# Attention pairs of a hybrid decoder step: a projection slot placed between the second and third transposes, transposes and value products regrouped in threes

## The reference

```python
h = jnp.einsum('btd,dc->btc', xn, w_in)           # the input projection, D_MODEL = 1024
# q, k, v of the attention: 16 query heads and 2 key/value heads of 64 columns
s = jnp.einsum('bnqhgd,bnshd->bnhgqs', qb, kk).astype(jnp.float32) * scale
s = s - alibi_slopes(B_QHEADS).reshape(B_KVHEADS, B_GROUP, 1, 1) * dist
s = jnp.where(valid[None, :, None, None], s, NEG)
p = sink_softmax(s, sinks)                         # softmax with one more logit per head
o = jnp.einsum('bnhgqs,bnshd->bnqhgd', p, vv.astype(jnp.float32))
hb = ob * jax.nn.silu(zb.astype(jnp.float32))      # gated by another projection
```

## Time and profile before

| what | value |
|---|---|
| median of 3 runs | 1328.07 us (1328.01 to 1328.28) |
| profiled execution, its own time | 1327.93 us |
| its span, first to last instruction | 1326.1 us |
| PE busy | 1290.7 us (97%) |
| DVE busy | 593.1 us (45%) |
| ACT busy | 516.7 us (39%) |
| mean granted PE clock | 0.986 of full speed |

### The profile page before, as it was taken

The page is one execution under the profiler, slowest core; times in us unless marked ns, Lnnn a source line. Parts: engine busy times, 40 slices in busy tenths (PEclk is TensorE's granted clock), DMA queues, the critical chain, the costliest instruction groups (busy, mean ns, idle before and its releaser), DMA issues.

```text
span 1326.1 us, 23484 instructions
## 1 busy us (share of the span) xinstructions
PE 1290.7 (97%) x9148; PEld 1224.2 (92%) x9148; DVE 593.1 (45%) x1237; ACT 516.7 (39%) x1019; POOL 260.7 (20%) x119
## 2 busy tenths in 40 slices
PE   4999999999999999999999999999999999999998
PEld 4999999999999999999999989889888899999885
DVE  6646657474746465600000155555555202345122
ACT  6453635445353535611111354555454324114111
POOL 0222221221322222212222201111110111342000
PEclk9999999999999999999999999999999899999999
DMA  6212121302021221111112211111100312241331
GB/s 197 66 33 66 35 64 34 79 18 79 24 73 47 66 65 35 46 50 47 47 47 52 69 33 32 32 32 32 32 16 1 106 32 64 56 104 32 114 127 38
DMA packets 136750, 73.61 MB, mean 56 GB/s; under 512 B 37185, under 2 KB 133138, under 8 KB 136690
## 3 DMA queue, kind: packets, MB, share of 16 engines
q1 hardware_dynamic: 136706, 72.99, 20.0%
HBM read 63.77 MB, written 10.22 MB: 56 GB/s over the span
## 4 chain that ended last, share of the span: by engine, by line
PE 54%; DVE 4%; issue 1%; ACT 0%; DVEq 0%; ACTq 0%
PE pj L968 36%; PE pj L984 3%; PE pj L1331 3%; DVE scores L1620 2%; PE ps_e L1208 1%; PE ps_a L1331 1%; PE ps_e L1331 1%; PE ps_d L1208 1%; PE ps_a L1169 1%; PE ps_c L1331 1%; PE ps_d L1331 1%; PE ps_b L1331 1%; DVE scores L1610 1%; PE ps_c L1196 1%; PE ps_a L1196 1%; PE ps_b L1196 1%
## 5 line engine op out<-in xcount | busy, mean ns | idle before, releaser
L968 PE MATMUL pj<-xn_h,w_h 128*128 128x352 f32 x1704 | 564.6, 331 | 4.5 <-DVE xn_l L1387 1.9
L968 PE MATMUL pj<-xn_h,w_l 128*128 128x352 f32 x1704 | 553.5, 325 | 0.0
L968 PE MATMUL pj<-xn_l,w_h 128*128 128x352 f32 x1704 | 553.0, 325 | 0.0
L558 POOL TENSOR_TENSOR w_l<-w_raw,w_h 128x1024 fp32r<-128x1024 f32 x82 | 203.2, 2477 | 695.9 <-ACT w_h L630 695.9
L968 PEld LDWEIGHTS pj<-xn_h,w_h 128*128 128x128 f32 x1704 | 325.3, 191 | 13.3 <-issue 3.4
L968 PEld LDWEIGHTS pj<-xn_l,w_h 128*128 128x128 f32 x1704 | 325.6, 191 | 0.2
L968 PEld LDWEIGHTS pj<-xn_h,w_l 128*128 128x128 f32 x1704 | 325.3, 191 | 0.0
L630 ACT ACTIVATE w_h<-w_raw 128x1024 fp32r<-128x1024 f32 x82 | 86.4, 1054 | 114.4 <-PE pj L968 100.1
L1568 DVE TENSOR_TENSOR mg<-sg,pj 128x352 f32 (+1 forms) x24 | 12.4, 521 | 151.9 <-PE pj L968 150.4
L835 ACT ACTIVATE scores<-scores,stat 128x256 f32<-128x256 f32 (+1 forms) x128 | 61.4, 480 | 0.0
L968 PE MATMUL pj<-hl_l,w_h 128*128 128x352 f32 x168 | 54.2, 323 | 0.0
(11 more groups left out here) (362 smaller groups left out, 2006.9 us busy)
## 6 DMA issues: line engine op xcount, KB each, us to landing
w_raw<-in_w_in_dram SPq DMA_DIRECT2D x132, 256.0 KB, 3.4
x_t<-in_x_prompt_dram SPq DMA_DIRECT2D x8, 512.0 KB, 9.4
s<-in_state_hgrn_dram SPq DMA_DIRECT2D x8, 512.0 KB, 4.2
out_dram<-s SPq DMA_DIRECT2D x8, 512.0 KB, 3.2
w_raw<-in_w_pa_dram SPq DMA_DIRECT2D x16, 256.0 KB, 3.0
w_raw<-in_w_pb_dram SPq DMA_DIRECT2D x16, 256.0 KB, 4.4
wo_raw<-in_w_out_dram SPq DMA_DIRECT2D x8, 512.0 KB, 3.8
x_o<-in_x_prompt_dram SPq DMA_DIRECT2D x8, 512.0 KB, 4.2
```

Of the source, the lines that this page charges most:

```text
L558: g.tensor_tensor(w_l[p][:], w_raw[p][:], w_h[p][:].bitcast(F32), ALU.subtract).then_inc(w_lo_ready, 1)
L968: mm = nc.tensor.matmul(pj[g][:, 0:W], w[:, kt, :], x[:, kt, span(g)], start=(kt == 0 and m == 0), stop=(kt == KT - 1 and m == 2))
```

## The change

On PE, the slot next2 goes between t1 and t2. Behind it stand t2, t3, t4, then o0, o1; behind gate0 o2, o3, o4 and t5, t6, t7; behind gate1 o5, o6, o7. Before, the order was t0 to t2, next2, o0, o1, t3, t4, gate0, o2, o3, t5, t6, gate1, o4, t7, o5 to o7. On DVE, pt1 goes ahead of the last quarter's normalisation, and h0 ahead of pt5. On ACT, the copy q2 goes ahead of pt2, and the rounding of weights stays ahead of pt4. No instruction is added or removed.

```diff
     softmax = (["qs"] + [x for k in quarters for x in units("t", k) + [f"nm0_{k}", f"nm1_{k}"]]
-               + [x for k in quarters for x in [f"dn{k}", f"rd{k}"] + units("n", k)] + ["zs"])
-    values = ["pt1", "pt3", "pt5", "h0", "pt7", "h1"]
+               + [x for k in quarters for x in (["pt1"] if k == 3 else []) + [f"dn{k}", f"rd{k}"] + units("n", k)] + ["zs"])
+    values = ["pt3", "h0", "pt5", "pt7", "h1"]
...
                 for n in range(0, NC, 2):
-                    if n == 4:
+                    if n == 2:
                         queries(2)
-                        if not last:
-                            split_hi(B(4))
+                    if n == 4 and not last:
+                        split_hi(B(4))
                     a.wait_ge(pe_done, pe.at(now, f"t{n}"))
...
-                for n in range(3):
+                turn(0)
+                turn(1)
+                next_slot(2)
+                for n in (2, 3, 4):
                     turn(n)
-                next_slot(2)
                 out(0)
                 out(1)
-                turn(3)
-                turn(4)
                 gate_slot(0)
-                out(2)
-                out(3)
-                turn(5)
-                turn(6)
+                for n in (2, 3, 4):
+                    out(n)
+                for n in (5, 6, 7):
+                    turn(n)
                 gate_slot(1)
-                out(4)
-                turn(7)
-                out(5)
-                out(6)
-                out(7)
+                for n in (5, 6, 7):
+                    out(n)
                 gate_slot(2)
...
-                for k in quarters:
-                    normalise(now, k, stat, QU * k, QU * (k + 1), scores, keys)
...
+                for k in quarters:
+                    if k == 3:
+                        copy_turned(1)
+                    normalise(now, k, stat, QU * k, QU * (k + 1), scores, keys)
...
-                copy_turned(1)
                 copy_turned(3)
+                gated_values(0)
                 copy_turned(5)
-                gated_values(0)
                 copy_turned(7)
                 gated_values(1)
```

More of the change, by code:

```diff
@@ L109, in hybrid_step @@
     softmax = (["qs"] + [x for k in quarters for x in units("t", k) + [f"nm0_{k}", f"nm1_{k}"]]
-               + [x for k in quarters for x in [f"dn{k}", f"rd{k}"] + units("n", k)] + ["zs"])
-    values = ["pt1", "pt3", "pt5", "h0", "pt7", "h1"]
-    turn_order = ["t0", "t1", "t2", "o0", "o1", "t3", "t4", "o2", "o3", "t5", "t6", "o4", "t7", "o5", "o6", "o7"]
+               + [x for k in quarters for x in (["pt1"] if k == 3 else []) + [f"dn{k}", f"rd{k}"] + units("n", k)] + ["zs"])
+    values = ["pt3", "h0", "pt5", "pt7", "h1"]
+    turn_order = ["t0", "t1", "t2", "t3", "t4", "o0", "o1", "o2", "o3", "o4", "t5", "t6", "t7", "o5", "o6", "o7"]
     norms = ["rl0", "rl1", "rls", "rx"]
@@ L126, in hybrid_step @@
         ("kv", each_slot("v") + each_slot("q") + ["vt0", "vts", "kt", "ks"] + each_slot("sigz"), 1, 0),
-        ("swa", exps + ["q0", "q1", "pt0", "pt2", "q2", "pt4", "pt6"] + each_slot("sigz"), HEADS - 1, 0),
+        ("swa", exps + ["q0", "q1", "pt0", "q2", "pt2", "pt4", "pt6"] + each_slot("sigz"), HEADS - 1, 0),
         ("swa_l", exps + ["pt0", "pt2", "pt4", "pt6"], 1, 0),
@@ L1632, in pair @@
                            lambda h: sink_m[:, h:h + 1], scores_next=k + 1)
-                for k in quarters:
-                    normalise(now, k, stat, QU * k, QU * (k + 1), scores, keys)
-                v.tensor_copy(z_s[:, bass.ds(m, 1), :], one(zb[:, SEQ:T])).then_inc(dve_done, dve.tick(now, "zs"))
-                if not last:
-                    slopes_of(now, m + 1)
                 def copy_turned(n):
@@ L1643, in copy_turned @@
                     v.tensor_copy(PT[:, n % 3, :, :].rearrange("p a q -> p (a q)"), (ps_a, ps_b, ps_c)[n % 3][:]).then_inc(dve_done, dve.tick(now, f"pt{n}"))
+                for k in quarters:
+                    if k == 3:
+                        copy_turned(1)
+                    normalise(now, k, stat, QU * k, QU * (k + 1), scores, keys)
+                v.tensor_copy(z_s[:, bass.ds(m, 1), :], one(zb[:, SEQ:T])).then_inc(dve_done, dve.tick(now, "zs"))
+                if not last:
+                    slopes_of(now, m + 1)
                 def gated_values(n):
```

## The result

The changed kernel takes 1321.57 us (median of 6 runs, 1319.99 to 1324.08), the kernel before 1328.17 us beside it. The ratio is 0.995, with a 95% interval of 0.994 to 0.9959: 6.6 us less, where 4.2 were forecast. The direction and the place were right, and the wait at t2 went as forecast; the prices of the regrouped work were not right, and the time lies 0.2 us under the range. Measured once more on another chip, it was 1320.65 us against 1328.15, a ratio of 0.9941 (0.9929 to 0.9953).

A forecast was written before the change was run, and what follows sets the result against it. PE, busy 97% of the span, was taken as the bound. Seven loop pairs at 0.53 us give 3.7, plus 0.5 for the last pair: 4.2 us less, so 1323.9 us, range 1321.8 to 1326.5.

The forecast's parts named there:

- pt1: On DVE, its early place ends 1.8 us before t4; in its old place t4 would wait about 0.3 us.
- (b): On PE from next2 to gate0: 1.79 us becomes 2.35 us, a loss of 0.56 us per pair.
- (c): On PE from gate0 to gate2: o4 beside o3 and t7 beside t6 gain 0.16 us per pair.
- (a): On PE from t1 to next2: with t2 moved behind the slot, 1.35 us becomes 0.42, a gain of 0.93 us.
- Sum per pair: Net gain over one attention pair of the loop: 0.53 us, with bounds 0.28 and 0.60.
- The upper bound, 0.60: Most that one loop pair could gain, in us, taking t4's price of 0.35 for t1 to the slot.
- (d): The last pair, which has no gate slots: 0.5 us gained, bounds 0 and 0.6, with o3 close to pt3.
- The tail: Behind o7 of the last pair: PE's 1.29 us idle, for the sigmoid that waits for h1, would stay.
- The clock: In the pairs granted clock 1.00 would stay, though the longest stretch without a slot grows from 2.7 to about 3.0 us.
- Rival D: Within the pairs the clock falls over longer stretches without a slot: 24.5 us slower if every loop pair; chance 0.08.
- Rival B: Behind the pairs the clock's fall changes length: 1322.2 us if shorter, 1325.7 if longer; chance 0.12.

The follow-up runs named there:

- e4: Changed kernel with value products and transposes alternating behind gate0 instead of grouped by kind; period of a loop pair 35.47 us against 34.87.
- e2: Changed kernel with t2 put back ahead of the slot next2, regrouping kept; period of a loop pair 35.37 us, against 35.75 in the kernel before.
- e1: Kernel before with only the slot next2 moved between t1 and t2; period of a loop pair 35.78 us against 35.75.
- e5: Kernel before with next2 between t1 and t2 and pt1 ahead of the last quarter, no regrouping; period of a loop pair 35.17 us against 35.75.
- e6: Changed kernel with h0 back behind pt5 on DVE; period of a loop pair 34.87 us, the same as the change.
- e7: Changed kernel with the cached values' transfer on its own semaphore, waited for ahead of the new tokens' value products; period 34.87 us, one run 1322.11 us.
- e8: Changed kernel with next2 between t0 and t1, later blocks regrouped, pt1 back in its old place, cached values on their own semaphore: 1317.79 us, ratio 0.992 to the kernel before.

## Why the prediction missed

The step that failed is the price list behind (b) and (c). The two together were forecast as 0.56 - 0.16 = 0.40 us lost per pair, and 0.42 - 0.36 = 0.06 were lost: that is 0.34 of the 0.35 us by which a pair was missed. (a), the wait at t2, was right.

- **(a) t1 to the slot, 0.93 us gained:** right. 1.35 us before, 0.42 after: 0.93.
- **(b) the slot to gate0, 0.56 us lost:** mis-sized. 0.42 was lost. The step that failed is the list of prices: "t3 starts at 811.57 and t4 at 812.07: 0.50 us" was taken as the price of a transposed block, but t3 stands behind a value product and pays 0.055 us for that in its first matmul (0.164 us to the second instead of 0.109). Behind a slot or another transpose a block is 0.44. The 0.86 us of o0 and o1 held 0.05 of waiting for pt1, which the waits did not list.
- **(c) gate0 to gate2, 0.16 us gained:** mis-sized most. It was 0.36. "0.51 for each" came from dividing the 1.53 us of o5 to o7 by three, and these hold an entry (0.05), an exit (0.10) and a wait of o7 for pt7 (0.07). Within a group a value block is 0.44. So putting o4 beside o3 and t7 beside t6 saves 0.15 per switch taken away, as e4 measures, plus the end of o7's wait.
- **Sum per pair:** 0.93 - 0.42 + 0.36 = 0.87, the timeline's 0.88. e2 shows the same from the other side: without the slot's new place the regrouping, with pt1's move in it, gives 0.38, where these prices gave 0.1. The upper bound, 0.60, was made from single rows of the same kind and shared their fault.
- **pt1:** right in its working and more important than it was said to be. e1 and e5 show that the slot's place is worth nothing without it.
- **(d) the last pair, 0.5 us:** it gave 0.88, too. o3 waits for pt3, as feared: it starts 0.60 us behind o2 instead of 0.44 and loses 0.05 more by starting again; against that, without gate slots between the groups the last pair had three switches in either direction before, and now has two from transposes to value products and one back.
- **The tail:** the 1.29 us of idle time behind o7 stayed to the hundredth. That the cached values would become late was not seen; 0.49 us.
- **The clock.** Rival D did not come: 1.00 in the pairs, with stretches of 816.93 - 814.19 = 2.74 us without a slot, no longer than the 2.7 of before and not 3.0. The Trainium skill, "TensorE: Matmul & The Clock Gate", section "A second HAM failure mode: psum-queue depth-cycling", tells of a kernel whose clock swung with short idle times between groups of matmuls that go round the PSUM banks. The trace shows none of it here: 1.00 over 204 us, before and after.
- **Rival B** did not come in the changed kernel, where the fall was as long as before, but the fall differs between profiles. In ten of the eleven the clock falls behind the pairs; 500 matmuls, counted from some 5 us behind the new tokens' scores, take 82.5 to 82.7 us of the trace where the fall lasts 6.8 us, 81.0 to 81.2 where it lasts 3.4 (e5, e6, e7 and e8), and 79.7 in e4, where there is none. The changed kernel had the long fall in both its profiles, like the kernel before. Without any edit the clock differs, too: of the 11 runs of the kernel before on one chip, the four with a mean granted clock of 0.983 took 1328.15 to 1330.41 us, the three with 0.986 or 0.987 took 1326.25 to 1327.84. The first pair's start varies by some 3 us, too (768.33 to 771.57 over the eleven profiles). The e8 window over the fall, to be held against the 0.57 above:

```profile
1044.00:1052.00 8.00, 8.00 (x45) 7.76 (x45) 0.43 (x1) 0.46 (x1) 2.36 (x1) 0.79 0.22 66
```

So the forecast was right in sign and in the wait that it removed, and too small by 0.35 us per pair, 2.8 us in eight, of which the cached values hid 0.5. The pairs' 7.0 us less that 0.49 is 6.5, the measured 6.6.

## What to carry to other kernels

The price of a block of small matmuls is not the length of its group divided by its number. Take the distance between two blocks in the middle of a group of the same kind, and price entry, exit and any hidden wait apart; distances between single matmuls show them. When work is moved out of a wait, look at what the next step waits for: here the place of one copy on DVE, 0.69 us long, made the difference between 0.58 us and nothing. And where a loop's stages repeat, its period in one profile tells hundredths of a microsecond that whole runs, with 2 us of their own noise, do not.

## What the runs showed of the hardware

Distances between matmul starts on PE at the full clock, the same in all eleven profiles to within 0.01 us (f32, 128 columns moving):

- transpose to transpose 0.109 us; two rows of value matmuls (128*64) start 0.007 us apart, and the next two 0.109 after the first.
- the first transpose after a value product or after a wait: 0.164 us to the second. The first two rows of value matmuls in a group, or after a wait: 0.05 us more, likewise.
- transpose to value product 0.20 us, value product to transpose 0.20, value product to slot 0.20, slot to value product 0.25, slot to transpose 0.16, transpose to slot 0.03. The 0.03 are not the whole price of that change: the slot's second matmul then starts 0.245 us behind its first, where the matmuls within a slot start 0.160 apart, so the two together, 0.11 us, are as much as one more transpose. Behind value products the slot's first step is 0.266.

A wait on PE of any length has this entry on top, and the profile's idle time counts neither it nor what the pipeline hides: 0.28 us were listed for t2, and 0.43 to 0.50 were lost.
